# A float32 transformer kernel: one weight slot in four gets its low part from GpSimd in the gate and up stages

## What is computed

```python
def swiglu(x, w_gate, w_up, w_down):
    return (jax.nn.silu(x @ w_gate) * (x @ w_up)) @ w_down

for i in range(DEPTH):                       # DEPTH = 2
    f = swiglu(rmsnorm(h, g[0]), ffn_w_gate[i, 0], ffn_w_up[i, 0], ffn_w_down[i, 0])
    h = h + FFN_RES_WEIGHT * rmsnorm(f, g[1])
    ...                                      # retention (i = 0) or stick-breaking attention (i = 1)
    f = swiglu(rmsnorm(h, g[4]), ffn_w_gate[i, 1], ffn_w_up[i, 1], ffn_w_down[i, 1])
    h = h + FFN_RES_WEIGHT * rmsnorm(f, g[5])
    gate = jax.nn.sigmoid(rmsnorm(h, g[6]) @ ple_w_gate[i])
    h = h + rmsnorm(gate * (p[i] @ ple_w_proj[i]), g[7])
```

## Time and profile before

| | |
|---|---|
| median of 3 runs | 1420.61 us (1420.31 to 1421.7) |
| span of the profiled execution | 1418.9 us |
| granted TensorE clock, mean | 0.998 |
| TensorE busy | 1386.3 us, 98% |
| VectorE busy | 846.0 us, 60% |
| ScalarE busy | 729.7 us, 51% |
| GpSimd busy | 62.0 us, 4% |
| low parts on VectorE | 460, 540.2 us busy, 1221 ns each |

### The profile page before, as it was taken

The page is one execution under the profiler, slowest core; times in us unless marked ns, Lnnn a source line. Parts: engine busy times, 40 slices in busy tenths (PEclk is TensorE's granted clock), DMA queues, the critical chain, the costliest instruction groups (busy, mean ns, idle before and its releaser), DMA issues.

```text
span 1418.9 us, 18949 instructions
## 1 busy us (share of the span) xinstructions
PE 1386.3 (98%) x6434; PEld 1139.3 (80%) x6434; DVE 846.0 (60%) x1066; ACT 729.7 (51%) x1026; POOL 62.0 (4%) x117
## 2 busy tenths in 40 slices
PE   6999999999999999999999999999999999999898
PEld 5888888888888888878888888878888878888676
DVE  5555666667565555575555544575554676677564
ACT  6444454444454444565444465564454565545683
POOL 0000010000010000010000000010000010002000
PEclk9999999999999999999999999999999999999999
DMA  7656555556646566456566454446666455555331
GB/s 234 194 186 206 177 164 192 175 187 204 197 144 193 178 200 230 141 173 190 188 206 228 141 178 142 150 152 192 191 215 218 156 178 179 179 173 172 127 99 60
DMA packets 186237, 251.41 MB, mean 177 GB/s; under 512 B 15508, under 2 KB 115388, under 8 KB 186172
## 3 DMA queue, kind: packets, MB, share of 16 engines
q1 hardware_dynamic: 186172, 250.56, 54.6%
HBM read 249.45 MB, written 1.05 MB: 177 GB/s over the span
## 4 chain that ended last, share of the span: by engine, by line
PE 88%; DVE 5%; ACT 3%; POOL 1%; issue 1%; DMA 0%; SPq 0%; POOLq 0%; ACTq 0%; DVEq 0%
PE sums L489 27%; PE sums L491 27%; PE sums L490 27%; DVE w_lo L1343 2%; PE turn L580 1%; POOL stat L898 1%; PE turn L527 1%; DVE xg L1357 1%; ACT x_hi L965 1%; DVE h L1381 1%; ACT junk L969 0%; PE turn L827 0%; ACT w_hi L953 0%; DMA raw<-in_ffn_w_up_dram 0%; DVE x_lo L1362 0%
## 5 line engine op out<-in xcount | busy, mean ns | idle before, releaser
L1343 DVE TENSOR_TENSOR w_lo<-raw,w_hi 128x1024 fp32r<-128x1024 f32 x460 | 540.2, 1221 | 182.7 <-ACT w_hi L953 181.4
L489 PE MATMUL sums<-w_hi,x_hi 128*128 128x512 f32 x1312 | 522.5, 398 | 9.7 <-DVE w_lo L1343 5.4
L953 ACT ACTIVATE w_hi<-raw 128x1024 fp32r<-128x1024 f32 x460 | 461.1, 1051 | 127.7 <-PE sums L491 73.4
L491 PE MATMUL sums<-w_hi,x_lo 128*128 128x512 f32 x1312 | 513.4, 391 | 0.0
L490 PE MATMUL sums<-w_lo,x_hi 128*128 128x512 f32 x1312 | 512.4, 391 | 0.0
L489 PEld LDWEIGHTS sums<-w_hi,x_hi 128*128 128x128 f32 x1312 | 247.4, 189 | 64.7 <-issue 14.6
L491 PEld LDWEIGHTS sums<-w_hi,x_lo 128*128 128x128 f32 x1312 | 247.0, 188 | 52.4
L490 PEld LDWEIGHTS sums<-w_lo,x_hi 128*128 128x128 f32 x1312 | 247.6, 189 | 49.9 <-issue 1.0
L489 PE MATMUL sums<-w_hi,y_hi 128*128 128x512 f32 x512 | 201.1, 393 | 1.0 <-DVE y_lo L1563 1.0
L491 PE MATMUL sums<-w_hi,y_lo 128*128 128x512 f32 x512 | 199.4, 389 | 0.0
L490 PE MATMUL sums<-w_lo,y_hi 128*128 128x512 f32 x512 | 199.3, 389 | 0.0
(11 more groups left out here) (169 smaller groups left out, 766.8 us busy)
## 6 DMA issues: line engine op xcount, KB each, us to landing
raw<-in_ffn_w_gate_dram SPq DMA_DIRECT2D x176, 256.0 KB, 3.8
raw<-in_ffn_w_up_dram SPq DMA_DIRECT2D x176, 256.0 KB, 4.7
raw<-in_ffn_w_down_dram SPq DMA_DIRECT2D x176, 256.0 KB, 3.8
raw<-in_ret_w_in_dram SPq DMA_DIRECT2D x96, 256.0 KB, 4.2
raw<-in_conv_w_in_dram SPq DMA_DIRECT2D x64, 256.0 KB, 4.0
raw<-in_attn_w_in_dram SPq DMA_DIRECT2D x64, 256.0 KB, 3.8
raw<-in_sb_w_in_dram SPq DMA_DIRECT2D x48, 256.0 KB, 3.5
raw<-in_ret_w_out_dram SPq DMA_DIRECT2D x32, 256.0 KB, 4.0
```

The costliest lines, as they stand in the source:

```text
L489: pe.matmul(bank[:, :], a, wh, start=(first and c == 0), stop=False, skip_group_check=True)
L491: mm = pe.matmul(bank[:, :], b, wh, start=False, stop=(last and c == SC - 1), skip_group_check=True)
L953: act.activation(w_hi[:, n % RING].rearrange("p c n -> p (c n)"), raw[:, n % RAW].rearrange("p c n -> p (c n)"), ACT.Copy).then_inc(hi_mad ...
L1343: dve.tensor_tensor(w_lo[:, n % RING].rearrange("p c n -> p (c n)"), raw[:, n % RAW].rearrange("p c n -> p (c n)"), w_hi[:, n % RING].rear ...
```

## The change

In the four gate and up stages, slots s0+3, s0+7, ... s0+47 (twelve per stage, the last being the fourth slot of the down matrix behind it) get their low part from GpSimd. They are 48 of the 460 slots. GpSimd runs the same subtraction on the same tile and raises a semaphore of its own, `lo_pool`. TensorE and the SP queue wait on `lo_pool` or `lo_made`, by the slot. In GpSimd's list the split of s0+3 stands behind `norm_post` of t = 0 (in the first stage behind `norm_in` of t = 0), the split of s0+7 behind `norm_in` of t = 1, and the other ten in a loop. VectorE does three splits where it did four.

```diff
+POOL_EVERY = 4
+FFN_AHEAD = 4 * FI + 4
+POOL_SLOTS = [PHASES[f"ffn_in{f}"].slot0 + 3 + POOL_EVERY * i for f in range(4) for i in range(FFN_AHEAD // POOL_EVERY)]
+
+def lo_count(n):
+    on_pool = sum(1 for q in POOL_SLOTS if q <= n)
+    return on_pool if n in POOL_SLOTS else n + 1 - on_pool
+
+def lo_step(n):
+    return 2 if n in POOL_SLOTS else RING - 2
...
+        def wait_lo(eng, n, j=None):
+            eng.wait_ge(lo_pool if n in POOL_SLOTS else lo_made, lin(lo_count(n), lo_step(n), j))
...
                 if n >= RAW:
-                    sp.wait_ge(lo_made, lin(n - RAW + 1, RING, j))
+                    wait_lo(sp, n - RAW, j)
...
-                pe.wait_ge(lo_made, lin(n + 1, RING, j))
+                wait_lo(pe, n, j)
...
-            for t in range(NT):
-                norm_in(0, t)
+            def split(n, j=None):
+                pool.wait_ge(hi_made, lin(n + 1, RING, j))
+                pool.tensor_tensor(w_lo[:, n % RING].rearrange("p c n -> p (c n)"),
+                                   raw[:, n % RAW].rearrange("p c n -> p (c n)"),
+                                   w_hi[:, n % RING].rearrange("p c n -> p (c n)").bitcast(F32),
+                                   ALU.subtract).then_inc(lo_pool, 1)
+
+            def ffn_splits(f):
+                s0 = PHASES[f"ffn_in{f}"].slot0
+                split(s0 + 7)
+                with pool.Fori(0, (FI - 1) // 2) as j:
+                    split(s0 + 11, j)
+                    split(s0 + 15, j)
+
+            norm_in(0, 0)
+            split(PHASES["ffn_in0"].slot0 + 3)
+            norm_in(0, 1)
+            ffn_splits(0)
+            before_ffn = {"ret_out": 1, "ple_gate0": 2, "sb_out": 3}
...
                 for t in range(NT):
                     if name in post:
                         norm_post(name, t)
+                    if t == 0 and name in before_ffn:
+                        split(PHASES[f"ffn_in{before_ffn[name]}"].slot0 + 3)
                     norm_in(b, t)
+                if name in before_ffn:
+                    ffn_splits(before_ffn[name])
...
             def split_to(n):
                 while split_next[0] < min(n, SLOTS):
-                    split(split_next[0])
+                    if split_next[0] not in POOL_SLOTS:
+                        split(split_next[0])
                     split_next[0] += 1
...
                     for s in range(2):
-                        for k in range(4):
+                        for k in range(3):
                             split(ph.slot0 + 8 + 4 * s + k, j)
```

More of the change, by code:

```diff
@@ L264, in build @@
         raw_loaded = [sem(f"raw_loaded{i}") for i in range(RAW)]
-        hi_made, lo_made = sem("hi_made"), sem("lo_made")
+        hi_made, lo_made, lo_pool = sem("hi_made"), sem("lo_made"), sem("lo_pool")
         slot_used, sums_done = sem("slot_used"), sem("sums_done")
```

## The result

The changed kernel takes 1424.02 us (median of 11 runs, 1422.15 to 1425.7), the kernel before 1420.61 us (11 runs, 1420.28 to 1421.9). The ratio is 1.0021, with a 95% interval of 1.0013 to 1.0029: 3.4 us, slower by about the least that a measurement of this kernel can tell. The forecast was 1423.9 us.

What follows compares the result with a forecast made beforehand. TensorE, busy 98% of the span, was taken as the bound. Terms 0 + 0 + 0 + 2.2 + 1.1 = +3.3 us on 1420.6 gave 1423.9 us, range 1419.5 to 1427.3.

Steps and rivals of the forecast that it cites:

- The cost of 0: 40 loop splits and four s0+7 splits: GpSimd's later finish is covered before TensorE uses the slot, cost 0.
- d: Duration of one GpSimd split, taken as 2.3 us, range 1.2 to 4 us; VectorE takes 1.22 us.
- the 3 us that I named as a sign of being wrong: GpSimd's split instruction lasting over 3 us would show the forecast wrong.
- Turns, not sharing: GpSimd's split holds a VectorE instruction with two SBUF inputs for its whole rest, instead of both running at a shared rate.
- Rival 2: VectorE is never held; xg at the border to ffn_in2 starts earlier: -1.1 us, 1419.5 us, chance 0.15.
- The border to `ffn_in3`: GpSimd's s0+3 split starts before VectorE's update of h and holds it, so TensorE waits: d - 0.1 = +2.2 us.
- The race of a tenth of a microsecond: At ffn_in3, GpSimd's split was to start ahead of VectorE's update of h, which started 0.11 us behind the power.
- The border to `ffn_in2`: GpSimd's s0+3 split gets in ahead of VectorE's third split, so xg is late: d - 1.16 = +1.1 us.
- the list of signs: Expected profile signs, among them TensorE's waits for h growing about 3 us, one over 2 us at ffn_in3.
- No clock to win back: TensorE in the first stage's loop is busy 120.00 of 120.00 us at full clock, so no clock to gain.
- rival 3: Loops: above d = 4.9 us each of 40 blocks pays d - 4.9; at d = 6, +44 us, 1465 us; chance 0.04.

Runs made afterwards that it cites:

- both_back: Changed kernel with s0+3 of ffn_in2 and of ffn_in3 split on VectorE again, 46 slots still on GpSimd: 1421.19 us.
- f3_twice: Changed kernel with GpSimd doing the split of s0+3 at the border to ffn_in3 twice, the second behind a wait for the first: 1427.61 us.
- f3_back: Changed kernel with only s0+3 of ffn_in3 split on VectorE again: 1422.09 us.
- after_again: The changed kernel run once more, unedited: 1423.77 us.
- moba_fill: Kernel before, with 9 and 7 unread matmuls ahead of the transposes of the first two heads in the block attention: 1419.38 us.
- later_moba_fill: Changed kernel with GpSimd's s0+3 splits at ffn_in2 and ffn_in3 made to wait, plus unread matmuls at two block attention waits: 1418.37 us.
- loop_thrice: Changed kernel with GpSimd doing every split in the loops three times, each repeat behind a wait: 1471.11 us.
- f3_fill: Changed kernel with nine unread matmuls ahead of TensorE's transposes for h at the border to ffn_in3: 1423.48 us.
- f2_back: Changed kernel with only s0+3 of ffn_in2 split on VectorE again, 47 slots on GpSimd: 1424.22 us.
- loop_twice: Changed kernel with GpSimd doing every split in the loops twice, the second behind a wait for the first: 1423.50 us.

## Why the prediction was right, step by step

**The bound and the loops.** TensorE waits 5.2 us for low parts after, 5.4 before, and is busy 120.00 of 120.00 us in the first loop, as before. The cost of 0 for the 40 splits in the loops and for those of s0+7 stands; both_back shows it.

**The duration.** d was taken as 2.3 us. Where GpSimd has to wait for nobody its split takes 2.35 to 2.41 us; the mean of 2.82 has the wait at a seam in it, and so has the longest, 3.02 us, just over the 3 us that I named as a sign of being wrong. The estimate of 2.25 us from the Trainium skill's page (GPSIMD Engine Reference, Performance versus the Vector engine) is 0.1 us short.

**Turns, not sharing.** The direction that no row of before showed is shown now: 2.76 us for the half of `h` that takes 0.75, GpSimd at full pace beside it, and two such holds in f3_twice. The Trainium skill (SBUF — State Buffer, SBUF: two separate sides) has it as a rule that of a GpSimd instruction and a VectorE instruction with two SBUF inputs, the one that starts first keeps the other out for the whole instruction. The trace agrees: 2.0 us of hold behind a split of 2.35. The trace adds what happened at the seams seen, at 615.8 and in f3_twice: the engine that waits gets in, though the other has more queued. Rival 2, VectorE never held, is out.

**The border to `ffn_in3`.** Forecast 2.2 us, measured 2.0 (TensorE's transposes at 926.24 against 923.31, less the 0.9 us by which the kernel was behind by then). The race of a tenth of a microsecond fell as forecast in every profile that has this placement. The split starts 0.03 us before the power has ended, here and in f3_twice (922.84 against 922.87). f3_back says 1.9.

**The border to `ffn_in2`.** Forecast 1.1 us, measured 1.0, and both_back says 0.9. One detail of the list of signs was wrong: I expected TensorE's waits for `h` to grow by 3 us, and they grew by 2.1. The microsecond of this border stands as a wait for `x_lo`, since that comes first.

**The sum.** 3.3 us forecast, 3.4 measured (2.7 in after_again), 3.0 in the held instructions. The sum lacked a term: a pause of TensorE can cost clock on top of itself, 1.4 and 1.6 us in two of the profiles. "No clock to win back" holds for the loops alone: in the block attention moba_fill won back 1.7 us of the kernel before. Two errors of a few tenths, stalls too large and clock left out, worked against each other. At this precision the forecast was also lucky.

**Rivals 2 and 3.** The price of rival 2, a gain of 1.1 us where VectorE isn't held, was right in kind: later_moba_fill has 1.0 us, though by another placement. The threshold of rival 3 was wrong. I put it at d = 4.9 us; the trace of loop_thrice has it at 6.4. The step that failed is the load: I added 0.9 us of issue to 4.7 us from issue to landing, and the raw buffer was full 3.63 us after its first issue. The issue of the second transfer overlaps the first, and the second had landed 3.2 us after its own issue at 107.92, against a median of 4.5 us in the same profile. It belongs to the first of four pairs issued in a row; that the median is long because of the pairs behind was not tested. The price of rival 3 was too high as well: by d - 4.9 for each of 40 blocks it would be 132 us at d = 8.2, and 47 were measured, since 13 of the blocks don't wait.

**What stays open.** f3_fill saved 0.3 us where 0.5 to 0.8 was expected, within what it can tell. How often the clock falls at the border to `ffn_in3` was not counted; it did in the profiles of f2_back, after_again and f3_twice and not in those of loop_twice and the changed kernel's first. What decides it was not found.

## What to carry to other kernels

An engine at 4% busy is not free: what it starts can hold its neighbour, and that counts wherever the neighbour stands on the path at that moment. Before moving work to GpSimd, look on VectorE's timeline for instructions with two operands in SBUF that the path waits for, and place GpSimd's instruction, with a wait if need be, beside those with an operand in PSUM. On a kernel that TensorE bounds at 98%, count its pauses rather than the busy time of the others; 46 of the splits moved were worth nothing, and the other two cost 3 us.

## What the runs showed of the hardware

- VectorE's instructions with two SBUF operands (`h`, `x_lo`, its splits) and GpSimd's split, which reads two tiles in SBUF, exclude each other for their whole length; 2.0 us of hold behind a split of 2.35. With one operand in PSUM VectorE isn't held: `hidden` at 0.48, `y_lo` at 0.69 and `xg` at 1.29 us beside GpSimd's split.
- By its records GpSimd starts an instruction that doesn't depend on the one before it ahead of that one's end: 923.28 against 923.31, and 922.84 against 922.87 in f3_twice.
- A pause of TensorE of 2.1 us is followed by half clock in some executions (1.4 us lost in after_again, 1.6 in f2_back) and not in others with the same program (after, 1.00). Two pauses close together, of 2.2 and 1.4 to 1.8 us, were followed by it in every profile that has them unfilled: 0.89 or 0.94 over 1315 to 1345 us, in loop_thrice, where they come later, 0.89 over 1370 to 1400. Sixteen matmuls without a use, put into them, made the kernel before 1.7 us faster.
